# Which queue issues the small parameter loads of a feed-forward stage: SyncE's or ScalarE's

## The reference

```python
h = rmsnorm(x, norm2_g[l])
u = causal_dwconv(h @ ffn_up[l], ffn_conv_w[l], ffn_conv_b[l])   # 3 taps per channel
u_gate, u_val = jnp.split(u, 2, axis=-1)
x = x + (jax.nn.gelu(u_gate) * u_val) @ ffn_down[l]
```

## Time and profile before

| what | value |
|---|---|
| median of 3 runs | 3399.34 us |
| lowest and highest | 3396.48 and 3399.64 us |
| the profiled execution, own time | 3396.45 us |
| its span in the trace | 3394.7 us |
| TensorE busy over the span | 3130.7 us, 92% |
| ScalarE busy | 1123.5 us, 33% |
| feed-forward stage in the trace | about 1484.9 to 2244 us |

### The profile page before, as it was taken

How to read it: one execution, slowest core, us unless ns; L and a number is a source line. 1 busy time by engine, 2 the same in 40 slices (tenths; PEclk the granted TensorE clock), 3 DMA queues, 4 the chain that set the end, 5 groups by cost and what they waited for, 6 DMA issues and landing times. The chain is left out here.

```text
span 3394.7 us, 40123 instructions
## 1 busy us (share of the span) xinstructions
PE 3130.7 (92%) x15115; PEld 2555.2 (75%) x15115; DVE 1425.9 (42%) x2254; ACT 1123.5 (33%) x1466; POOL 754.4 (22%) x482
## 2 busy tenths in 40 slices
PE   8998899899989799979999999968799999999988
PEld 6776777678867587767888878847687888878766
DVE  4355133311135421143443343454434465555766
ACT  4344133321146521132322222232232445324332
POOL 2000100022211122111212211242423233123333
PEclk9999999999999899979999999979699999899979
DMA  3100210022221112232111111125031311222223
GB/s 127 49 23 7 63 32 29 10 59 65 62 49 42 46 56 74 87 51 72 48 39 43 58 47 37 31 87 93 10 87 47 100 38 32 100 45 69 75 81 118
DMA packets 275400, 194.00 MB, mean 57 GB/s; under 512 B 66504, under 2 KB 246856, under 8 KB 275280
## 3 DMA queue, kind: packets, MB, share of 16 engines
q1 hardware_dynamic: 273168, 191.33, 19.9%
q10 hardware_dynamic: 2112, 1.05, 0.1%
HBM read 165.77 MB, written 26.57 MB: 57 GB/s over the span
## 5 line engine op out<-in xcount | busy, mean ns | idle before, releaser
L136 POOL TENSOR_TENSOR w_low<-w_raw,w_high 128x1024 fp32r<-128x1024 f32 (+1 forms) x178 | 411.0, 2309 | 1846.6 <-ACT w_high L129 1842.2
L154 PE MATMUL pu<-act_high,w_high 128*128 128x512 f32 x704 | 276.5, 393 | 12.3 <-POOL w_low L136 8.6
L154 PE MATMUL pu<-act_low,w_high 128*128 128x512 f32 x704 | 276.1, 392 | 0.0
L154 PE MATMUL pu<-act_high,w_low 128*128 128x512 f32 x704 | 275.9, 392 | 0.0
L129 ACT ACTIVATE w_high<-w_raw 128x1024 fp32r<-128x1024 f32 (+1 forms) x178 | 177.2, 996 | 275.1 <-PE py L154 92.8
L154 PE MATMUL pg<-act_high,w_high 128*128 128x512 f32 x512 | 202.1, 395 | 28.6 <-ACTq L615 24.3
L154 PE MATMUL pg<-act_low,w_high 128*128 128x512 f32 x512 | 201.0, 393 | 0.0
L154 PE MATMUL pg<-act_high,w_low 128*128 128x512 f32 x512 | 200.5, 392 | 0.0
L639 DVE TENSOR_TENSOR gate<-gate,py 128x1024 f32<-128x1024 f32 x24 | 29.3, 1222 | 389.7 <-PE py L154 389.7
L154 PEld LDWEIGHTS pu<-act_high,w_high 128*128 128x128 f32 x704 | 133.5, 190 | 41.2 <-POOL w_low L136 9.3
L1631 DVE TENSOR_TENSOR x<-x,pd 128x512 f32<-128x512 f32 x176 | 118.1, 687 | 93.8 <-PE pd L1560 93.8
(11 more groups left out here) (640 smaller groups left out, 7509.8 us busy)
## 6 DMA issues: line engine op xcount, KB each, us to landing
w_raw<-in_w_in SPq DMA_DIRECT2D x106, 512.0 KB, 4.1
w_raw<-in_ffn_up SPq DMA_DIRECT2D x44, 512.0 KB, 3.8
w_raw<-in_w_out SPq DMA_DIRECT2D x24, 512.0 KB, 4.5
v_raw<-in_ffn_down SPq DMA_DIRECT2D x11, 1024.0 KB, 5.0
decay<-acum_rows SPq DMA_DIRECT2D x16, 512.0 KB, 3.7
x_ring<-in_x SPq DMA_DIRECT2D x8, 512.0 KB, 9.5
m_part<-gate SPq DMA_DIRECT2D x8, 512.0 KB, 3.0
w_raw<-in_w_br_rnn SPq DMA_DIRECT2D x8, 512.0 KB, 6.2
```

The costliest lines, as they stand in the source:

```text
L136: pool.tensor_tensor(self.low[slot][:, 0:nk, :], self.raw[slot][:, 0:nk, :], self.high[slot][:, 0:nk, :].bitcast(F32), ALU.subtract).then_ ...
L154: last = pe.matmul(out[:, h, :] if not halves else out[h], w[slot][:, k, :], x[:, k, cols], start=(n == 0), stop=(n == 3 * nk - 1))
```

## The change

The 18 small transfers of the stage (three taps, the bias, four of `c`, six of `lam`, four of `b`) are issued by ScalarE ahead of its first wait, in that order. SyncE issues only the weight tiles. Sizes, layouts, destinations and semaphores stay the same, and so does all computation. `load` and `load_c` have their argument renamed from `sp` to `queue`.

```diff
             @block.sync
             def _(sp):
-                for j in range(3):
-                    sp.dma_start(taps[:, j, :], per_channel(io["ffn_conv_w"][0, j])).then_inc(sem("small"), 16)
-                sp.dma_start(bias[:, :], per_channel(io["ffn_conv_b"][0])).then_inc(sem("small"), 16)
                 def turn(i):
                     for j in range(G):
                         W.load(sp, 0, i * G + j, up[:, bass.ds((i * G + j) * P, P)])
                         W.load(sp, 1, i * G + j, up[:, bass.ds((i * G + j + FCH) * P, P)])
                         if j == 0:
                             V.load(sp, 0, i, down[bass.ds(i * (G * P), G * P), :])
-                S5.load_c(sp)
                 turn(0)
-                S5.load(sp)
                 with sp.Fori(1, NG) as i:
                     turn(i)
...
             @block.scalar
             def _(act):
+                for j in range(3):
+                    act.dma_start(taps[:, j, :], per_channel(io["ffn_conv_w"][0, j])).then_inc(sem("small"), 16)
+                act.dma_start(bias[:, :], per_channel(io["ffn_conv_b"][0])).then_inc(sem("small"), 16)
+                S5.load_c(act)
+                S5.load(act)
                 act.wait_ge(sem("small"), 64)
```

More of the change, by code:

```diff
@@ L3146, in __init__, with load @@
         self.core, self.sem, self.T = core, sem, T
-    def load(self, sp):
+    def load(self, queue):
         io, sem, T = self.core.io, self.sem, self.T
@@ L3152, in load, with load_c @@
             half = slice(r * S5_P, (r + 1) * S5_P)
-            sp.dma_start(T.lam[half, 0, :], two("s5_lambda_re_2")[r]).then_inc(sem("lam"), 16)
-            sp.dma_start(T.lam[half, 1, :], two("s5_lambda_im_2")[r]).then_inc(sem("lam"), 16)
-            sp.dma_start(T.lam[half, 2, :], io["s5_log_step_2"][0].rearrange("(q r) -> r q", r=2)[r].partition_broadcast(S5_P)).then_inc(sem("lam"), 16)
+            queue.dma_start(T.lam[half, 0, :], two("s5_lambda_re_2")[r]).then_inc(sem("lam"), 16)
+            queue.dma_start(T.lam[half, 1, :], two("s5_lambda_im_2")[r]).then_inc(sem("lam"), 16)
+            queue.dma_start(T.lam[half, 2, :], io["s5_log_step_2"][0].rearrange("(q r) -> r q", r=2)[r].partition_broadcast(S5_P)).then_inc(sem("lam"), 16)
         for i, name in enumerate(("s5_b_re_2", "s5_b_im_2")):
             for r in range(2):
-                sp.dma_start(T.B[r * S5_P:(r + 1) * S5_P, i, :, :], io[name][0].rearrange("(q r) p h -> r p q h", r=2)[r]).then_inc(sem("b"), 16)
-    def load_c(self, sp):
+                queue.dma_start(T.B[r * S5_P:(r + 1) * S5_P, i, :, :], io[name][0].rearrange("(q r) p h -> r p q h", r=2)[r]).then_inc(sem("b"), 16)
+    def load_c(self, queue):
         io, sem, T = self.core.io, self.sem, self.T
@@ L3163, in load_c @@
             for r in range(2):
-                sp.dma_start(T.cn[:, i, :, r, :], io[name][0].rearrange("(n g) h p -> (g h) n p", g=8)).then_inc(sem("c"), 16)
+                queue.dma_start(T.cn[:, i, :, r, :], io[name][0].rearrange("(n g) h p -> (g h) n p", g=8)).then_inc(sem("c"), 16)
     def on_pe(self, pe, pC):
```

## The result

The changed kernel takes 3418.2 us (median of 4 runs, 3416.74 to 3421.85); the kernel before, run beside it and counted with its earlier runs, 3397.91 us. The ratio is 1.0062 with a 95% interval of 1.0045 to 1.0080, so the kernel became 0.6% slower, by 20.3 us. The forecast was 3416 us with a range of 3404 to 3424.

The account below looks back on a forecast made before the run. TensorE's two `w_low` waits, 8.6 us together, were taken to bound the feed-forward stage. TensorE restarts 24.1 us later, saves 8.6 and waits 0.9 more: +16.3 us, forecast 3416 us, range 3404 to 3424.

Parts of the forecast that it names:

- main step: Feed-forward stage start: 18 issues hold ScalarE, with `u_gate`, splits and TensorE's `project(0, 1, 0)` behind them; chance 0.74.
- Ta: Time when ScalarE has issued all 18 transfers and is free for `u_gate`: taken as 1532, bounds 1527.6 and 1538.3.
- slow clock: TensorE's lower clock level after a wait; one slow restart remains, its 96 matmuls taking 23.66 us as before.
- second gap: TensorE's 6.13 us wait before `project(1, 0, 0)` goes, with its slow restart: 8.6 us saved.
- wait for VectorE: TensorE waits before `output(0)` for VectorE's first sum, since S5 work ends later: 0.9 us new.
- sum of 46.7 us: The 18 transfers' issue times on SyncE added up: taps and bias 11.17, `c` 5.33, `lam` 18.80, `b` 11.40.
- plain sum: Stage start plus issue times and small gaps, 1484.92 + 46.7 + 0.5, puts ScalarE free at 1532.1.
- The one engine: The two `log_step` transfers run one after the other on about one DMA engine, whose backlog holds back issue.
- lower bound of 1527.6: Earliest time for ScalarE to be free, if weights on their own queue cost the small transfers nothing: 1533.8 - 6.2.
- The break-even: ScalarE free before 1516.6 means the change gains, after it loses; the difference is Ta - 1516.6.
- ScalarE is hardly held: Rival: 18 issues on ScalarE take only 6.6 us, then it waits for the bias; 3387 to 3392 us, chance 0.11.
- the stalls belong to SyncE's queue: Rival: `lam` and `b` issue without stalls on ScalarE, free at 1508.1 to 1514.3; 3392 to 3398 us, chance 0.08.

Follow-up runs that it names:

- e1: Kernel before, all transfers left on SyncE, ScalarE kept busy by 46 copies ahead of its first wait: 3419.24 us, ratio 1.0067.
- e3: Changed kernel with the two `log_step` transfers replaced by one of 128 pieces of 128 bytes: 3400.90 us, ratio 1.0013.
- v1: Kernel before, everything on SyncE's queue, with only `log_step` made one transfer of 128 pieces of 128 bytes: 3393.59 us, ratio 0.9993.
- e2: Changed kernel with taps and bias put back on SyncE; `c`, `lam` and `b` stay on ScalarE: 3407.81 us, ratio 1.0035.
- e4: Kernel before with only taps and bias moved to ScalarE's queue: 3413.97 us, ratio 1.0049.
- v5: e4 with `log_step` as one transfer of 128 pieces of 128 bytes on SyncE: 3398.14 us, ratio 1.0004.
- v6: v2 with VectorE's first S5 step cut in two, second part behind group 1, powers and `b` one group later: 3382.17 us, ratio 0.9958.
- v4: v2 with the S5 work of ScalarE and VectorE one group later: 3384.58 us, ratio 0.9971.
- v2: v1 with the first loads on SyncE reordered, first weight tile ahead of `c`: 3388.07 us, ratio 0.9974.
- e5: Changed kernel with the S5 work of ScalarE and VectorE one group later: 3420.70 us, ratio 1.0069.

## Why the prediction was right

Its main step, ScalarE held by the 18 issues with all else behind them, is what the trace shows and what e1 confirms alone. Its terms, each against the stage's start (1484.92 before, 1484.38 after):

| term | forecast, us | measured, us |
|---|---|---|
| ScalarE free (Ta) after the stage's start | 47.1 | 49.9 (1534.32 - 1484.38) |
| from Ta to TensorE's start | 4.75 | 4.63 (1538.95 - 1534.32) |
| TensorE's restart later than before, both from the stage's start | 24.1 | 26.8 (54.57 - 27.76) |
| slow clock after that restart, against before | 0 | +0.45 |
| second gap with its slow clock | -8.6 | -8.6 |
| wait for VectorE | +0.9 | +2.9 (7.6 now, 4.7 in the same list before) |
| sum | 16.3 | 21.5 |

The stage as measured, from its first issue to the last sum into `x`, grew by 21.3 us (1484.38 to 2264.93 after, 1484.92 to 2244.15 before), and the span by 21.5, so next to nothing is left for the other stages. The medians differ by 20.3.

**How near it came.** The growth was forecast as 16.3 us and was 20.3. That 3416 lies only 2.2 us under the measured time is in part luck: I had counted from a median before of 3399.34 us, which came down to 3397.91 with one more run.

**Ta.** This is the larger of the two terms that were too small: TensorE's restart came 2.7 us later than forecast. The sum of 46.7 us came to 49.1, and its parts moved more than the whole. Taps and bias took 18.2 us instead of 11.2, with the weights beside them; `lam` took 14.3 instead of 18.8, with no weights ahead of it. I had bracketed the stretch with 6.2 us: it was 7.0, and 4.5 came back. That the two nearly cancel is what the plain sum needed, and the forecast had only an argument for it.

**The one engine.** That `log_step` holds the last 20 us of the issue is right: without it the hold is 18.8 us shorter (e3). The lower bound of 1527.6 rested on the weights costing the rest nothing, and they did cost.

**The slow clock.** After 27.6 us of idle the ten steps from 1538.95 to 1543.38 took 4.43 us, at the granted clock of this window (the columns are those of the earlier trace rows):

```profile
1538.95:1543.38 4.43, 4.43 (x10) 0.50 0.41 118
```

Before, they took 3.98 us at 0.57. So the forecast's 0 was 0.45 us too low. What a restart loses does not go by the length of the wait: 1.7 us after 2.50, 2.7 after 4.28 (v1), 2.3 after 6.13, 2.8 after 9.20 (e3), 1.5 after 20.21 (e2) and 2.2 after 27.60. A forecast can take 1.5 to 2.8 us for one, and not one fixed value.

**VectorE.** This is the second term that was too small, 2.9 us for 0.9. The time of S5's step was taken from a stretch in which it met no `split_low`; once it ends as TensorE starts `output(0)`, it meets one and takes 2.15 us longer.

**The break-even.** The slow clock and VectorE moved it. For e3 the forecast's rule gives -0.5 + 0.9 = +0.4 us. In its trace the slow clock holds for 13 steps from 1520.68 to 1526.39, 5.71 us where the normal pitch makes 2.95, so it loses 2.8 us and not 1.7; VectorE's wait is 7.6 us as in the changed kernel, 2.0 more than forecast; and behind that wait the clock falls, as in v1, and costs 2.9 us more, a term that the forecast has not at all. That makes +6.4 us, and the stage grew by 6.5 from TensorE's first product to its last (763.97 against 757.46 us). The whole kernel grew by only 4.3 us, since the stages behind were some 2 us shorter in this trace than in that of the kernel before, with the same code; that much is noise.

**The rivals.** That ScalarE is hardly held is wrong: its 18 issues take 2.7 us on average. That the stalls belong to SyncE's queue is wrong too: 7.53 and 7.54 us stand in ScalarE's rows where 7.59 and 7.58 stood in SyncE's. A slower pace on ScalarE is wrong by the same rows and by the bias, 3.72 against 3.71 us. The rule of the Trainium skill cited with the first rival (page "DMA: Bandwidth & Descriptors", section "Issuing engines are not separate DMA queues"), that initiating a transfer costs little beside the transfer, is not what this case shows: the bias took 3.72 us to issue and 8.7 us to land. The page says 'usually', and these pieces of 4 bytes are outside of that.

## What to carry to other kernels

The time in which a sequencer issues its transfers is part of that engine's work. Before transfers move to an engine that computes, add up their issue times and look at what that engine does first: a wait covers only issues that must land for it anyway. When a transfer of a few KB takes over 10 us, look at how many DMA engines work on it and change the transfer, not its queue: here that edit, an order and a cut in VectorE's work were together worth 14.8 us (the edit alone nothing that can be told), and the move cost 20.3. And when a gap closes, ask what was being done in it.

## What the runs showed of the hardware

- While a transfer of 1024 pieces of 4 bytes with a broadcast source was under way, the mean DMA share stood at 0.04 to 0.05, about one engine of 16 (changed kernel, 1512 to 1520), and two of them landed 11.3 us apart there (1522.0 and 1533.3). The same values as 128 pieces of 128 bytes landed 3.7 us after their issue began, and 1024 pieces of 4 bytes without a broadcast 2.9 to 3.0 us (both e3).
- Such a transfer in one queue holds back transfers of the other queue: the bias landed 28.5 us (e4) and 25.0 us (e2) after its issue began, 12.0 us without it (v5), and 9.0 us with all in one queue.
- ScalarE's sequencer issued these transfers at SyncE's pace: 3.72 against 3.71 us for the bias, 11.38 against 11.40 us for `b`.
- A VectorE operation with two SBUF operands that began 0.11 us after one of GpSimd took 2.46 us instead of 0.31. It took 2.43 to 2.46 us in the changed kernel and in all ten kernels here but v6, where VectorE's step was cut.
- After the same wait of 2.9 us TensorE's granted clock was 1.00 in the changed kernel, e4, v4 and v5 and fell to its lower level in v1, v2, e3 (2.8 to 2.9 us lost) and e1, e2, e5 (1.6 us lost).
